# A hybrid decoder layer on one core: constant products in TensorE's start, one low part earlier, a shorter reciprocal square root

## The reference, cut to what matters

```python
def _rmsnorm(x, w):
    xf = x.astype(jnp.float32)
    y = xf * lax.rsqrt(jnp.mean(xf * xf, axis=-1, keepdims=True) + EPS)
    return y * w.astype(jnp.float32)
...
    mod = jax.nn.silu(c) @ ada_w + ada_b
    shift, scale, gate = jnp.split(mod, 3, axis=-1)
    hn = (_rmsnorm(x, pre_w) * (1.0 + scale[:, None]) + shift[:, None]).astype(x.dtype)
    z = hn @ w_in
    xa, ga, q, fr, iv, gb = jnp.split(
        z, [D_A, 2 * D_A, 2 * D_A + D_B, 2 * D_A + 2 * D_B, 2 * D_A + 3 * D_B], axis=-1)
...
    ob = _rmsnorm(ob, onorm_w.reshape(N_HEADS_B, DV_B))
...
    m = jnp.concatenate([ya, yb], axis=-1).astype(x.dtype) @ w_out
    x = x + (gate[:, None] * _rmsnorm(m, post_w)).astype(x.dtype)
```

## Time and profile before

| what | value |
|---|---|
| median of three runs | 996.0 us (995.4 to 997.31) |
| the profiled execution, its own time | 996.84 us |
| its span, first to last instruction | 995.1 us |
| busy in the span: PE, DVE, ACT, POOL | 926.3, 676.6, 515.5, 149.5 us |
| mean granted clock of PE | 0.975 |

### The profile page before, as it was taken

The page is one execution under the profiler, slowest core; times in us unless marked ns, Lnnn a source line. Parts: engine busy times, 40 slices in busy tenths (PEclk is TensorE's granted clock), DMA queues, the critical chain, the costliest instruction groups (busy, mean ns, idle before and its releaser), DMA issues. The chain is left out here.

```text
span 995.1 us, 20265 instructions
## 1 busy us (share of the span) xinstructions
PE 926.3 (93%) x7822; PEld 668.3 (67%) x7822; DVE 676.6 (68%) x1901; ACT 515.5 (52%) x1050; POOL 149.5 (15%) x208
## 2 busy tenths in 40 slices
PE   5698967999999999999999999999999999999987
PEld 3455856568665867587757775786668675867554
DVE  3455788847784787568774878577847875687445
ACT  2634679443853476337733584438533863366321
POOL 4000010201130113011201112001301130111112
PEclk9797997999999999999999999999999999999998
DMA  9995202100110011001010011001101010100413
GB/s 312 323 310 169 85 2 86 64 1 23 43 64 2 23 43 65 1 22 43 26 41 23 1 44 65 2 23 43 65 1 44 1 51 1 44 1 29 117 43 114
DMA packets 46619, 61.15 MB, mean 61 GB/s; under 512 B 2748, under 2 KB 40208, under 8 KB 46524
## 3 DMA queue, kind: packets, MB, share of 16 engines
q1 hardware_dynamic: 46524, 59.86, 18.4%
HBM read 48.90 MB, written 10.95 MB: 60 GB/s over the span
## 5 line engine op out<-in xcount | busy, mean ns | idle before, releaser
L404 PE MATMUL ring<-hnh,wih 128*128 128x256 bf16 (+1 forms) x1152 | 290.9, 264 | 3.1 <-DVE wil L1348 3.1
L404 PE MATMUL ring<-hnh,wil 128*128 128x256 bf16 (+1 forms) x1152 | 290.7, 263 | 0.6 <-issue 0.6
L404 PE MATMUL ring<-hnl,wih 128*128 128x256 f16 (+1 forms) x1152 | 290.7, 263 | 0.0
L404 PE MATMUL ring<-woh,work 128*128 128x512 f16 x512 | 162.1, 379 | 0.0
L404 PEld LDWEIGHTS ring<-hnh,wih 128*128 128x128 f16 x1152 | 110.7, 98 | 14.7 <-issue 3.1
L404 PEld LDWEIGHTS ring<-hnh,wil 128*128 128x128 bf16 x1152 | 110.5, 98 | 13.1 <-issue 0.7
L404 PEld LDWEIGHTS ring<-hnl,wih 128*128 128x128 f16 x1152 | 110.5, 98 | 12.8
L873 ACT ACTIVATE qh<-qq 128x256 bf16<-128x256 f32 x96 | 41.5, 432 | 142.7 <-PE lev L404 83.0
L404 PE MATMUL ring<-wih,hnh 128*128 128x512 f16 (+1 forms) x264 | 100.1, 379 | 0.0
L404 PE MATMUL ring<-wih,hnl 128*128 128x512 f16 (+1 forms) x264 | 100.1, 379 | 0.0
L404 PE MATMUL ring<-wil,hnh 128*128 128x512 bf16 (+1 forms) x264 | 100.1, 379 | 0.0
(11 more groups left out here) (327 smaller groups left out, 1887.5 us busy)
## 6 DMA issues: line engine op xcount, KB each, us to landing
xin<-in_x_prompt_dram SPq DMA_DIRECT2D x16, 512.0 KB, 3.8
work<-in_x_prompt_dram SPq DMA_DIRECT2D x16, 512.0 KB, 4.6
out_dram<-work SPq DMA_DIRECT2D x16, 512.0 KB, 2.6
work<-in_ada_w_dram SPq DMA_DIRECT2D x5, 1024.0 KB, 11.3
wol<-in_w_in_dram SPq DMA_DIRECT2D x5, 1024.0 KB, 9.0
woh<-in_ada_w_dram SPq DMA_DIRECT2D x4, 1024.0 KB, 13.2
woh<-in_w_in_dram SPq DMA_DIRECT2D x4, 1024.0 KB, 10.8
work<-in_w_out_dram SPq DMA_DIRECT2D x4, 1024.0 KB, 5.5
```

What stands on the lines that cost most here:

```text
L404: last = mm(out, a(k), b(k), start=start and k == ks[0] and j == 0, stop=stop and k == ks[-1] and j == 2)
```

## The change

Three things are changed. PE gets a helper, `busy(bank, count)`, that multiplies constants (the identity as weights, `siluc` as the moving side, 256 columns, f32) into the second half of a bank that no engine reads at that time; it stands 27 times in the start: twice behind the first, third, fifth and seventh `ada`, twice ahead of the third and the fifth, seven times ahead of the seventh, twice behind the eighth and six times ahead of the first body. The results are overwritten or never read. On DVE, `rest(0)` moves from in front of the last `hn_rest` to behind the third. And `rsqrt_steps` takes nine operations: a first guess in one operation, one round with a polynomial of degree two, and one Newton round with the scale folded into its constants.

```diff
-NEWTON = 12
+NEWTON = 9
...
+RC0, RC1, RC2 = 1.87661677, -1.25213721, 0.375520627
...
+            def busy(bank, count):
+
+                for _ in range(count):
+                    mm(bank[:, 256:512], ident[:, :], siluc.rearrange("p k s -> p (k s)"), start=True, stop=True)
+
             for b in range(4):
                 if b > 1:
                     pe.wait_ge(mod_sb, b - 1)
-                ada(2 * b, (lev[0], ring[1])[b % 2])
-                ada(2 * b + 1, (lev[0], ring[1])[b % 2])
+                bank = (lev[0], ring[1])[b % 2]
+                if b:
+                    busy(bank, 7 if b == 3 else 2)
+                ada(2 * b, bank)
+                busy(bank, 2)
+                ada(2 * b + 1, bank)
+                if b == 3:
+                    busy(lev[0], 2)
...
+            busy(lev[0], 6)
             pe.wait_ge(wg_ld, 64)
...
                 done(V.tensor_scalar(v, ssq, 1.0 / count, EPS, ALU.mult, ALU.add))
-                done(V.tensor_scalar(t.bitcast(I32), v.bitcast(I32), 1, None, ALU.logical_shift_right))
-                done(V.tensor_scalar(y.bitcast(I32), t.bitcast(I32), -1.0, MAGIC, ALU.mult, ALU.add))
-                for _ in range(3):
-                    done(V.tensor_tensor(t, y, y, ALU.mult))
-                    done(V.scalar_tensor_tensor(t, t, -0.5, v, ALU.mult, ALU.mult))
-                    done(V.scalar_tensor_tensor(y, t, 1.5, y, ALU.add, ALU.mult))
+                done(V.tensor_scalar(y.bitcast(I32), v.bitcast(I32), -0.5, MAGIC, ALU.mult, ALU.add))
+                done(V.tensor_tensor(t, y, y, ALU.mult))
+                done(V.tensor_tensor(t, t, v, ALU.mult))
+                done(V.scalar_tensor_tensor(t, t, RC1 / RC2, t, ALU.add, ALU.mult))
+                done(V.scalar_tensor_tensor(y, t, RC0 / RC2, y, ALU.add, ALU.mult))
+
+                done(V.tensor_tensor(t, y, y, ALU.mult))
+                done(V.scalar_tensor_tensor(t, t, -0.5 * RC2 ** 3, v, ALU.mult, ALU.mult))
+                done(V.scalar_tensor_tensor(y, t, 1.5 * RC2, y, ALU.add, ALU.mult))
...
-                if j == 3:
+                hn_rest(0, j)
+                if j == 2:
                     rest(0)
-                hn_rest(0, j)
```

## The result

The changed kernel takes 986.24 us (median of 4, 985.25 to 987.01) beside 996.49 for the kernel before (median of 4, 995.4 to 997.31): ratio 0.9897, 95% interval 0.988 to 0.9914. Forecast was 987.5. The profiled execution of after took 987.01 us, of which its span is 985.3; the one of before 996.84 and 995.1.

A forecast was written before the change was run, and what follows sets the result against it. PE bounds the long middle, idling there for `kl`; its time before the first body and the DVE chains it awaits can be won. 996.84 - 2.4 - 6.4 = 988.0 profiled, 987.2 against the median, forecast 987.5, range 984 to 993.

The forecast's parts named there:

- 2.4 for the start: Start up to the first body's 48 products: they end at 48.2 where the 49th stood at 50.57, gaining 2.4 us.
- 6.4 for the square roots: All square-root chains, nine operations instead of twelve: 0.6 us saved per chain, together 6.4 us where it reaches PE.
- rival 4: First body: shifted work misses a fall of PE's clock in the fourth or seventh slice; up to 4 us more, 983; chance 0.07.
- the walk: PE's queue in the start, followed step by step with added products: clock rises at 20.9, first 48 products end at 48.2.
- the row of before: Trace of `turn_x` in the start: f32 products against the identity raised PE's clock; eight transposes took 1.95 us, then 1.59.
- The chains of `x_norm`: DVE chains for the next body, reaching PE's 1.09 us waits in bodies 0 to 6: 7 x 0.6 = 4.2 us won.
- The 0.5 forecast for the wait: PE's 1.09 us wait for `kl` behind `x_norm` in bodies 0 to 6: 0.5 us of each remains.
- The others: Chains outside `x_norm`: decode rows in body 7 0.5 us, `rows(0,1)` 0.6, two at the end 1.1; other `rows`, `x_out` nothing.
- the 1.75 forecast: PE's 2.35 us wait for `gbs` at 170.30, behind `rows(0,1)`: falls by 0.6 to near 1.75 us.
- 1 (the start gives nothing): Start: the clock rises late or falls again in a gap between products; 989.6 us, chance 0.16.
- 2 (ACT sets the 1.09): Body waits of 1.09 us stay because ACT's table loads and gates set them, not DVE; 991.9 us, chance 0.08.
- 3 (products do not raise the clock): Start: at 1.2 GHz the products only delay PE's queue, body 17.5 us late; 1007 us, chance 0.06.

The follow-up runs named there:

- The 33 products: Changed kernel plus 33 products of the identity with itself on PE, sized to the first body's gaps: 983.16 us, ratio 0.9873.

## Why the prediction was right, step by step

**The sum.** Forecast 2.4 for the start and 6.4 for the square roots; measured by medians 3.0 and 6.0. The rest of the 10.25 us between the medians, some 1.2, agrees with the earlier clock that the traces show at the second gates (1.27), part of rival 4, which had 0.07. The two traces divide alike: of their 9.83 us 2.77 are there at the first wait for `kl`, 1.27 come with that clock, and 5.8 are left for the square roots. The tenths are not shown: each start varies by 0.5 to 1.1 us at `kl`, and the 1.27 is one run against one run. The forecast missed by 1.3 us, about the clock that it left to rival 4. The 33 products won 3.1 us more in the stretches that rival 4 named.

**The start: the walk was right, its reason wrong.** The walk's steps stand in the trace: the clock rose at 20.1 to 21.6 (taken 20.9), `turn_mod(3)` ended at 40.04 (40.2), the six products at 42.7 (42.95), the 49th product ran at 47.81 (48.2). The step that failed is where the prediction has the gain come from: its walk lets the products raise the clock, pays for them by it, and takes the fast first products as the 2.4 us won, while the move is only said to cost nothing and has no term of its own. PE stood idle for 3.08 us until `rest(0)`; moving that is enough (3.0 us at the first wait for `kl` without a product), and products enough to make the clock full are paid for in full, and at `kl` by 0.7 more, by the time PE spends on them. Products without the move win about 0.9 there, one trace. So the 2.3 that both together show at `kl` meets the 2.4 of the walk because the walk held both edits, and not for the reason given. The prediction walked one queue with both edits in it and never walked it with one.

On the clock: two products of a constant, four instructions from 8.89 to 10.9, were followed by an `ada` at 1.07 us, 2.4 GHz, before the gap from 12.14 to 14.56, and the transposes of `turn_x` ran 16 in 2.0 us. The Trainium skill, "TensorE: Matmul & The Clock Gate", Part 4 (PE-mode transpose), against which the prediction kept the row of before, is contradicted here again: no sign of a transpose that keeps PE at 1.2 GHz. The prediction said more than its rows hold, though: that these transposes raised the clock. It rose while they ran, behind other f32 work without a gap from 22.25, and in the changed kernel it was full before they began.

**The chains of `x_norm`: right.** 7 x 0.6 = 4.2 forecast, 3.9 measured. The waits went from 1.09 only to 0.71 in most bodies though PE's landmarks moved by 0.6 a body. The other 0.2 lay in a gap too short for the list: in the fourth body the level before the wait began 0.34 behind the product ahead of it (458.15 and 458.49), after the change 0.11 (452.55 and 452.66). The 0.5 forecast for the wait was wrong, the time won was not. In the second body the wait is 1.06; DVE has a gap of 0.44 there that the profile gives no cause for. All ten traces with nine operations everywhere have it, the four others do not, and no run shows why.

**The others: 2.2 forecast, 2.1 measured** by medians, 1.35 between the profiled runs. At the end the wait went from 3.56 to 3.00, as forecast. `rows(0,1)` brought its 0.5 (166.32 to 165.82 between two runs level until then; the gap of 0.44 in the next body takes 0.3 of it back). But beside the earlier trace rows the wait fell by 0.1 only, because DVE lost more to POOL at that place. The kernel before had lost 0.76 there, one operation that took 0.92 instead of 0.16:

```profile
166.59 0.92 DVE L1183 TENSOR_TENSOR stat<-stat 128x4 f32<-128x4 f32 x1
```

The changed kernel lost 0.88 + 0.47 = 1.35, so 0.59 more, which is the 0.6 won:

```profile
158.78 2.14 DVE L1388 SCALAR_TENSOR_TENSOR wol<-work,par,woh 128x256 bf16<-128x256 f32 x4
...
161.98 1.05 DVE L1193 TENSOR_SCALAR stat<-stat 128x4 f32<-128x4 f32 x1
```

```profile
158.18 1.27 POOL L1696 TENSOR_TENSOR ii<-ii,xc 128x512 f32<-128x512 f32 x1 [13.02 <-ACT ii L955]
161.96 1.04 POOL L1699 TENSOR_TENSOR xc<-aa 128x512 f32<-128x512 f32 x1 [2.51 <-ACT aa L961]
```

In the run without products, where POOL's first product ran at 155.60 and DVE had nothing to do then, the same DVE rows read

```profile
157.70 1.67 DVE L1382 SCALAR_TENSOR_TENSOR wol<-work,par,woh 128x256 bf16<-128x256 f32 x4
...
160.42 0.17 DVE L1187 TENSOR_SCALAR stat<-stat 128x4 f32<-128x4 f32 x1
161.02 0.92 DVE L1190 TENSOR_TENSOR stat<-stat 128x4 f32<-128x4 f32 x1
```

with the loss of the kernel before, and PE waited 1.76 for `gbs`, the 1.75 forecast. The collision moves with the clock: in all three traces POOL's first product begins 7.12 to 7.14 us behind PE's second gates and the four operations of DVE 2.13 or 2.14 behind unit (1,1), and the clock sets the time between gates and unit.

**The rivals.** 1 (the start gives nothing) fell with the run that has the old start; 2 (ACT sets the 1.09) with the nine operations in `x_norm` alone, which win 3.9; 3 (products do not raise the clock) by the `ada` of 1.07 us at 10.84.

## What to carry to other kernels

Where one edit holds two remedies for one stall, walk the queue with each alone: here a reordering of one line did what 27 added products were credited with. A forecast on TensorE needs its clock in every stretch behind an idle gap; products of constants sized to such gaps took 3.1 us off this kernel, while 78 of them, reaching past the end of the gaps, made it 4.5 us slower. Before moving work that frees a buffer, look at which transfer waits for that buffer: 4.1 us later there cost 4.7 in all.

## What the runs showed of the hardware

- The same instructions, with the same gaps, got PE's clock back at different times: granted 0.63 and 0.88 over the same 14 us, worth 2.2 us some 12 us later.
- A DVE operation of four columns took 1.05 us instead of 0.17 when it began 0.02 us behind the start of a POOL product of 1.04 us, and another 0.92 in the run without products (POOL's product ran from 160.88 there); each ended 0.02 or 0.03 us behind POOL's. Four operations with two inputs in SBUF took 2.14 instead of 1.67. The Trainium skill, "SBUF — State Buffer", "SBUF: two separate sides", has GpSimd and certain DVE instructions (two inputs in SBUF, or a mode that uses both pairs of ports) lock one pair of ports, the first for its whole instruction while the other waits; these durations agree with it. No run varied POOL's work by itself.
- An f32 product of 128 columns is two instructions on PE and took 0.23 us at full clock for nearly all of them (5.97 us for 26), 0.29 where the clock was at half in the beginning (7.66 for 26).
